# Token tiles one column later, an earlier load, and expert lists kept in SBUF: three edits in an encoder block

## The reference, cut to what matters

```python
mixed = sigmoid(g_a) * (o_g @ w_o_gqa) + sigmoid(g_b) * (o_m @ w_o_mla)
h = h + mixed @ w_out
t = rmsnorm(h, ffn_norm)
aff = softmax(t @ w_router, axis=-1)            # 16 experts
g, idx = top_k(aff.T, 130)                      # each expert picks 130 tokens
xs = t[idx]
y = (silu(xs @ w_gate) * (xs @ w_up)) @ w_down  # hidden width 512
h = h.at[idx].add(y * g[..., None])
```

## Time and profile before

| what | value |
|---|---|
| median of the runs (lowest, highest) | 2949.36 us (2943.27, 2949.93) |
| the profiled execution's own time | 2949.2 us |
| its span, first to last instruction | 2947.4 us |
| TensorE busy | 2790.1 us, 95% |
| VectorE, ScalarE, GpSimd busy | 61%, 49%, 25% |
| mean granted TensorE clock | 0.972 of full speed |
| mixing, last pass ends; residual; selection; experts begin | about 1931, to 2178, to 2225, 2242 us |

### The profile page before, as it was taken

One profiled execution on the slowest core, in us unless ns is written; L12 is line 12 of the kernel. 1 busy time (PEld: TensorE's weight loads), 2 busy tenths in 40 slices (PEclk: granted clock), 3 DMA queues, 4 the chain that ended last, 5 costly groups with the idle time before them and its releaser, 6 DMA issues. The chain is left out here.

```text
span 2947.4 us, 54402 instructions
## 1 busy us (share of the span) xinstructions
PE 2790.1 (95%) x19748; PEld 2613.7 (89%) x19748; DVE 1811.8 (61%) x2888; ACT 1448.8 (49%) x2623; POOL 740.9 (25%) x1279
## 2 busy tenths in 40 slices
PE   8999899999999999999999999999946999999994
PEld 7888698999989999999999999988836999999994
DVE  6777766888887777775343334423354565555555
ACT  4333336888887777776222223311122445444543
POOL 0000013444442554546000000000031333323331
PEclk9999898999999999999999999999977999999997
DMA  6556493112204334553865754556645898888977
GB/s 210 154 157 191 143 385 111 49 47 73 52 23 101 90 100 127 138 148 104 239 183 162 212 161 136 143 180 195 198 126 138 203 211 200 201 198 215 204 160 266
DMA packets 534413, 466.64 MB, mean 158 GB/s; under 512 B 61907, under 2 KB 467107, under 8 KB 534257
## 3 DMA queue, kind: packets, MB, share of 16 engines
q1 hardware_dynamic: 510768, 403.68, 47.9%
q0 software_dynamic: 21120, 60.81, 9.1%
q10 hardware_dynamic: 2368, 0.16, 0.0%
HBM read 320.29 MB, written 144.21 MB: 158 GB/s over the span
## 5 line engine op out<-in xcount | busy, mean ns | idle before, releaser
L2835 PE MATMUL e_gu<-e_x_hi,w_hi 128*128 128x260 f32 x1024 | 294.2, 287 | 0.9 <-DVE e_x_lo L3040 0.9
L2835 PE MATMUL e_gu<-e_x_lo,w_hi 128*128 128x260 f32 x1024 | 290.3, 284 | 0.0
L2835 PE MATMUL e_gu<-e_x_hi,w_lo 128*128 128x260 f32 x1024 | 290.0, 283 | 0.0
L3035 DVE TENSOR_TENSOR w_lo<-w_raw,w_hi 128x2048 fp32r<-128x2048 f32 x90 | 206.3, 2292 | 100.5 <-ACT w_hi L2936 99.7
L1956 ACT ACTIVATE n_exps<-n_st_ps 128x348 f32<-128x348 f32 (+3 forms) x432 | 199.0, 461 | 120.5 <-PE n_st_ps L1901 116.0
L2039 DVE TENSOR_TENSOR n_p_lo<-n_exps,n_p_hi 128x696 fp32r<-128x696 f32 (+1 forms) x192 | 176.3, 918 | 106.4 <-ACT n_p_hi L1970 106.1
L123 POOL MEMSET s_ident<- 128x128 f32 x1 | 0.2, 209 | 779.2 <-POOLq L3247 779.2
L2835 PEld LDWEIGHTS e_gu<-e_x_hi,w_hi 128*128 128x128 f32 x1024 | 194.1, 190 | 1.1 <-DVE e_x_lo L3040 1.1
L2835 PEld LDWEIGHTS e_gu<-e_x_lo,w_hi 128*128 128x128 f32 x1024 | 194.3, 190 | 0.0
L2835 PEld LDWEIGHTS e_gu<-e_x_hi,w_lo 128*128 128x128 f32 x1024 | 193.9, 189 | 0.0
L2236 PE MATMUL c_acc<-c_tokens,c_w_back 128*128 128x260 f32 x1536 | 191.2, 284 | 2.9 <-DVE c_prod L2311 2.8
(11 more groups left out here) (344 smaller groups left out, 7751.0 us busy)
## 6 DMA issues: line engine op xcount, KB each, us to landing
c_raw<-in_w_in SPq DMA_DIRECT2D x64, 512.0 KB, 5.2
w_raw<-in_w_gate SPq DMA_DIRECT2D x64, 512.0 KB, 6.5
w_raw<-in_w_up SPq DMA_DIRECT2D x64, 512.0 KB, 8.0
w_raw<-in_w_down SPq DMA_DIRECT2D x64, 512.0 KB, 4.5
c_tokens<-hn_t SPq DMA_DIRECT2D x16, 1040.0 KB, 9.6
c_tokens<-o_t SPq DMA_DIRECT2D x32, 520.0 KB, 6.6
r_mt<-mix_t SPq DMA_DIRECT2D x32, 512.0 KB, 5.2
mix_t<-c_out_hi SPq DMA_DIRECT2D x32, 260.0 KB, 2.1
```

The lines of the kernel that those rows point to most:

```text
L2835: ins = pe.matmul(gu[:, j % 2, a, 0:W], w[:, j, at:at + P], t[:, k, :], start=(k == 0 and q == 0), stop=(k == DK - 1 and q == 2))
L3035: dve.tensor_tensor(w_lo[:, j, :], raw[:, j % RAW, :], w_hi[:, j, :].bitcast(F32), ALU.subtract)\
```

## The change

It has three parts. In the experts, column m of the down product is followed by tile m + 1 for m from 1 to 6, on TensorE, ScalarE and VectorE; the places of the late slabs stay as they were.

In mixing and residual, SP's wait for the last stores is taken out of mixing. Residual's SP waits for mixing's last product instead, loads mixed tile and `x` of tile 1, then `x` of tile 0, the gain row and the router, and only then waits for the stores.

For the lists, a tensor `aff_home` of 64 half lists of 528 columns lies at a fixed place of SBUF through residual and selection. The first halves hold the meta tokens and four tiles, the second halves four tiles and 16 columns that GpSimd sets to -1. List tiles of the steps before step 11 still go to `aff_t`; at step 11 SP waits for those stores and issues four DMAs that bring them home; the later tiles are stored straight into `aff_home`. The selection has no load of the lists, and VectorE waits for `row_map` only behind the 17 rounds.

```diff
 mix, SP:
-            sp.wait_ge(stored, 32 * DK * PASSES)
...
 residual, SP:
+            def load_home(s):
+                for g in range(GROUPS):
+                    tiles = (s - g + 1) // 2
+                    sp.wait_ge(aff_stored[g], 16 * tiles)
+                    late = (tiles - XCH // 2) * P
+                    back = (GROUPS + g) * E
+                    sp.dma_start(aff_home[g * E:(g + 1) * E, META:], scr["aff_t"][g * E:(g + 1) * E, META:FIRST_HALF])\
+                        .then_inc(gain_loaded, 16)
+                    sp.dma_start(aff_home[back:back + E, 0:late],
+                                 scr["aff_t"][g * E:(g + 1) * E, FIRST_HALF:FIRST_HALF + late]).then_inc(gain_loaded, 16)
+
+            sp.wait_ge(*mixed_done["products"])
+            load(1, 1)
             load(0, 0)
-            load(1, 1)
             sp.dma_start(gain[:, :], spread(io["ffn_norm"][0, :], 0, P)).then_inc(gain_loaded, 16)
             sp.dma_start(router[:, :, :], io["w_router"][0].rearrange("(k p) e -> p k e", p=P)).then_inc(router_loaded, 16)
+            sp.wait_ge(*mixed_done["stored"])
...
+                    if isinstance(s, int) and s == DIRECT:
+                        load_home(s)
...
+                    elif isinstance(s, int) and s >= DIRECT:
+                        first, at = (GROUPS + g) * E, (tile_index(s, g) - XCH // 2) * P
+                        sp.dma_start(aff_home[first:first + E, at:at + P], aff_rows[:, g, :]).then_inc(aff_stored[g], 16)
...
+            pool.wait_ge(router_loaded, 16)
+            pool.memset(aff_home[GROUPS * E:, XCH // 2 * P:], -1.0).then_inc(router_loaded, 1)
...
 choose, SP and VectorE:
-            for part in range(2):
-                sp.dma_start(aff[part * LISTS:(part + 1) * LISTS, :], scr["aff_t"][:, part * HALF:(part + 1) * HALF])\
-                    .then_inc(loaded, 16)
...
-            dve.wait_ge(loaded, 48)
...
             link(dve.tensor_copy(column[:, :], index[:, :]))
+            dve.wait_ge(loaded, 16)
...
 experts, TensorE:
-                    if not is_last(e) and m + 2 < DK:
-                        tokens_of(e + 1, m + 2)
+                    if not is_last(e) and 1 <= m < DK - 1:
+                        tokens_of(e + 1, m + 1)
...
 experts, ScalarE and VectorE, in both alike:
-                    if m + 2 < DK:
-                        tokens(e + 1, m + 2)
+                    if 1 <= m < DK - 1:
+                        tokens(e + 1, m + 1)
                     if m in LATE_SLABS:
                         slab(e + 1, LATE_SLABS[m])
```

More of the change, by code:

```diff
@@ L2343, in _, with residual @@
                     body(DK - 1, 1, True)
-    return dict(products=(prod_done, NB * DK * PASSES), first_products=(prod_done, NB * DK * PASSES - 1),
+    return dict(stored=(stored, 32 * DK * PASSES), products=(prod_done, NB * DK * PASSES), first_products=(prod_done, NB * DK * PASSES - 1),
                 out_weights=(out_split_lo, DK))
-def residual(nc, io, scr, block, ident, w_out, loads, mixed_done, passed):
+AFF_AT = 226304
+def residual(nc, io, scr, aff_home, block, ident, w_out, loads, mixed_done, passed):
     N = STEPS
@@ L2399, in residual @@
         LOADS = 16 * 2
+        DIRECT = N - 6
         @block.sync
@@ L2440, in body @@
                     wait_alone(sp, at_copied, s + 1, sp_passed)
+                    if isinstance(s, int) and s == DIRECT:
+                        load_home(s)
                     if isinstance(s, int) and s == N - 1:
                         for gg in range(GROUPS):
-                            sp.dma_start(scr["aff_t"][gg * E:(gg + 1) * E, 0:META],
+                            sp.dma_start(aff_home[gg * E:(gg + 1) * E, 0:META],
                                          aff_rows[:, g, gg * META:(gg + 1) * META]).then_inc(aff_stored[g], 16)
+                    elif isinstance(s, int) and s >= DIRECT:
+                        first, at = (GROUPS + g) * E, (tile_index(s, g) - XCH // 2) * P
+                        sp.dma_start(aff_home[first:first + E, at:at + P], aff_rows[:, g, :]).then_inc(aff_stored[g], 16)
                     else:
@@ L2454, in _ @@
             sp.wait_ge(aff_stored[1], 16 * (N // 2))
+            sp.wait_ge(gain_loaded, 16 + 32 * GROUPS)
+            sp.wait_ge(router_loaded, 17)
+        @block.gpsimd
+        def _(pool):
+            pool.wait_ge(router_loaded, 16)
+            pool.memset(aff_home[GROUPS * E:, XCH // 2 * P:], -1.0).then_inc(router_loaded, 1)
         @block.tensor
@@ L2573, in _, with choose @@
             steps(dve, body, 1, 3)
-def choose(nc, io, scr, rows_t, gates_t, out_rows, w_raw, w_hi, w_lo):
+FIRST_HALF = META + TOK // 256 * P
+def choose(nc, io, scr, aff, rows_t, gates_t, out_rows, w_raw, w_hi, w_lo):
     LISTS = GROUPS * E
     ROUNDS = (CAP + 7) // 8
-    HALF = TOK // 2
     with ExitStack() as ctx:
@@ L2588, in sem @@
             return nc.alloc_semaphore("s_" + name)
-        aff = sb("aff", [2 * LISTS, HALF])
         top, index = sb("top", [2 * LISTS, ROUNDS * 8]), sb("index", [2 * LISTS, ROUNDS * 8], U32)
@@ L3239, in row_map @@
     front = np.stack([x_offset, meta_offset - x_offset], axis=1)
-    back = np.stack([x_offset + TOK // 2, 0 * x_offset], axis=1)
+    back = np.stack([x_offset + FIRST_HALF, 0 * x_offset], axis=1)
     return np.concatenate([front, back]).astype(np.float32)
@@ L3245, in build @@
     scr = scratch_tensors(nc)
+    aff_home = nc.alloc_sbuf_tensor_at("aff_home", [2 * GROUPS * E, FIRST_HALF], F32, offset=AFF_AT)
     with nc.cleanup_on_exit(), ExitStack() as ctx:
@@ L3262, in build @@
         mixed_done = mix(nc, io, scr, block, mix_loads, attended, w_out, residual_loads, passed)
-        residual(nc, io, scr, block, ident, w_out, residual_loads, mixed_done, passed)
+        residual(nc, io, scr, aff_home, block, ident, w_out, residual_loads, mixed_done, passed)
     with ExitStack() as ctx:
@@ L3271, in build @@
         w_lo = weights.at((RAW + SLABS) * SLAB, "w_lo", [P, SLABS, SLAB], F32R)
-        choose(nc, io, scr, rows_t, gates_t, out_rows, w_raw, w_hi, w_lo)
+        choose(nc, io, scr, aff_home, rows_t, gates_t, out_rows, w_raw, w_hi, w_lo)
         experts(nc, io, scr, outs, rows_t, gates_t, out_rows, weights, w_raw, w_hi, w_lo)
```

## The result

The changed kernel takes **2983.51 us** (median of four runs, 2980.45 to 2985.53) against 2949.14 for the kernel before in the same comparison (2943.27 to 2949.93). The ratio is 1.0119, 95% interval 1.0102 to 1.0135: it is slower by some 35 us. The profiled execution took 2984.78 us for a span of 2983.0, against 2949.2 and 2947.4 before.

The account below looks back on a forecast made before the run. TensorE, busy 95% of the span, was taken as the bound. Experts + 21.3, residual - 6.15 and selection - 2.2 made + 12.9 us on 2949.4, forecasting 2962 us, range 2953 to 2983.

Parts of the forecast that it names:

- the clock: At 14 expert boundaries, a fall behind the new wait was priced at nothing; the other end was + 20.4 us.
- The clock falls too: Rival: clock falls at most of the 14 expert boundaries, + 13 to + 20 us more, 2975 to 2983; chance 0.30.
- The wait at the gate product: At 14 expert boundaries, TensorE waits 1.97 us for tile 7's x_lo, queued behind slab 4; each boundary grows by 1.55.
- + 18 to + 25: Range in us for the 14 expert boundaries together, with every release 0.05 to 0.1 quicker or slower; central value + 21.7.
- The boundary into the last expert: The 15th boundary: slab 4 starts earlier, so the copy of column 7 comes sooner, - 0.4 us.
- Residual: Second mixed tile loaded earlier, removing TensorE's wait and the clock's fall: - 6.15 us, at least - 2.5.
- the rival of 2.5: Rival in residual: the early load does not help, giving back only 2.5 us, total 2966; chance 0.07.
- its sign: In residual, the forecast itself expected the second split to start without a wait and at full clock.
- Selection: First max no longer waits for lists, - 2.79 us; wider passes cost at most + 0.54; together - 2.2.
- Sum: Whole kernel: experts + 21.3, residual - 6.15, selection - 2.2, together + 12.9 us, giving 2962.
- Tile 7 is hidden anyway: Rival at expert boundaries: gate product does not wait, each boundary gains 0.42 us, total about 2935; chance 0.06.

Follow-up runs that it names:

- Experiment 2: Changed kernel with 14 useless products behind column 7, filling TensorE's wait before the gate product: 2963.87 us, ratio 1.0064.
- the experts' order alone: Kernel before the change with only the later order of the token tiles in the experts: 2988.41 us, ratio 1.0146.
- experiment 3: Changed kernel with 5 useless products behind column 7, filling part of TensorE's wait before the gate product: 2964.78 us, ratio 1.006.
- experiment 1: Changed kernel with slab 4 moved from m = 5 to m = 6, behind tile 7: 2935.24 us, ratio 0.9964; timed again 2936.78 us.
- experiment 6: Experiment 1's kernel with slabs 4 and 5 of the last expert split in that expert, behind the results: 2934.64 us, ratio 0.9962.
- experiment 7: Experiment 6's kernel with the fourth hidden tile ahead of row squares, first roots and first normalized row: 2935.95 us, ratio 0.996.
- the experts' order undone: Changed kernel with the old order of token tiles in the experts, keeping early load and lists in SBUF: 2938.51 us, ratio 0.9973.
- selection alone: Kernel before the change with only the lists in SBUF: 2944.09 us, ratio 0.9996.
- residual alone: Kernel before the change with only the early loads of mixing and residual: 2942.11 us, ratio 0.9985.

## Why the prediction was wrong, point by point

The direction and the place were right, the time was 21.5 us too low (2962 against 2983.5), just beyond the upper end of 2983.

**The step that failed is the clock.** The prediction said of it: "A wait of 1.97 is nearer to that one, so I price the fall at nothing". Measured: 12 falls at 14 boundaries, 1.50 each against the 1.46 worked out from the earlier trace rows, and a thirteenth at the last boundary for 0.34, together 18.3 us. Experiment 2 shows this by itself: with the wait filled and the gate product no sooner, that time goes. The rival "The clock falls too" (2975 to 2983) was what happened; its price was right, its chance too low. The argument by the nearest row failed because one row of each kind (2.35 with a fall, 2.04 without) was taken to give a length from which the clock falls, and a wait below the row without a fall was then called safe. The 2.04 wait was a single event, and it gives no such length: ahead of the same transposes a wait of 2.07 in the changed kernel, and of 2.06 in the experts' order alone, was followed by half clock. Why 2.04 was not stays open. The Trainium skill, "TensorE: Matmul & The Clock Gate", section "HAM oscillation", tells of a loop whose DMA waits, some 3 to 5 us long, bring the clock down anew in every tile. The runs show the same for a wait that returns with every expert and is shorter, 1.87 to 1.89, in 12 of 14, and not for the 1.27 of experiment 3.

**The wait at the gate product** was right: predicted 1.97, measured 1.87, at all 14. From T2, T5 was forecast 5.48 later and came 5.45 later, T6 7.22 and 7.24, and x_lo of tile 7 stood 4.87 behind T6 as forecast. The boundary grew by 1.79, not 1.55: 0.12 at T2, which comes later behind the rest of column 1, and 0.10 in the steps behind it, most of it the release from x_lo to the gate product, 0.66 for 0.58. Over 14 boundaries that is 25.1, the upper end of "+ 18 to + 25".

**The boundary into the last expert** was forecast at - 0.4. Where no fall lies in its period (experiments 2 and 3) that period is 48.14 against 48.39 before: - 0.25.

**Residual** was right by the trace: 6.30 for the forecast 6.15 between the first and the third product of a mixed tile. The run of that part alone gives 4.4 with 6.15 inside its interval; the rival of 2.5 is inside it too, but its sign (a wait for `r_mt`) is absent from the trace.

**Selection**: forecast - 2.2 (- 2.8 to - 1.5), by the trace - 1.8; the stores into SBUF, taken at 0, cost 0.5 at the barrier (4.29 against 3.79).

**Sum.** With the measured terms: 14 x 1.79 + 18.3 - 0.25 - 6.3 - 1.8 = + 35.0, for a span 35.6 longer. Two differences outside these terms nearly cancel: residual is reached 2.3 later, and what follows the last gate product is 1.3 shorter. "Tile 7 is hidden anyway", the rival on the other side, forecast about 2935 for slab 4 out of the way; experiment 1, which puts it out of the way, measured 2935.24. That the two agree so well is luck: the rival was 14.7 less than before, and experiment 1 is 10.5 less than its own runs of before. A full boundary gained 0.35 instead of 0.42, and the last one lost 1.8 where - 0.4 was taken.

## What to carry to other kernels

When a step is moved along in a program with in-order queues, look at what the move puts ahead of it on the engine that releases the bound: here one entry of a dictionary, unchanged, came to stand between a tile and the product that waits for it, and one edit of it was worth 46 to 48 us. A new wait that returns with every pass has two prices, the wait itself and the clock behind it; take in both unless waits of that length at such a place are seen many times without a fall. And an operation taken out of one queue position has to be followed to its next one: experiments 6 and 7 won 5 us at a boundary, and lost 3 of them in the one and as good as all in the other behind the next queue.

## What the runs showed of the hardware

The length of a wait does not by itself say whether the clock falls. Waits of 1.87 to 1.89 were followed by half clock at 12 of 14 boundaries in both kernels that have them, and the two spared, six boundaries apart, had waits as long. A wait of 1.27 at the same place was not followed by it, at any of 14 boundaries. At the boundary into the last expert 2.07 and 2.06 were followed by it in the same two kernels, and 2.04 ahead of the same transposes kept full clock before the change, with the experts' order undone, in selection alone and in residual alone:

```profile
2856.55 1.06 PE L2851 MATMUL e_tp<-e_ident,e_y_t 128*65 128x128 f32 x8 [2.04 <-issue]
...
2859.69 1.09 PE L2851 MATMUL e_tp<-e_ident,e_y_t 128*65 128x128 f32 x8 [1.21 <-ACT e_y L2966]
```

```profile
2856.00:2858.00 2.00, 1.45 (x14) 1.48 (x15) 1.97 (x3) 0.44 (x1) 0.15 (x1) 1.00 0.00 0
2858.00:2860.00 2.00, 0.79 (x8) 0.54 (x7) 1.96 (x4) 1.04 (x2) 0.00 (x0) 1.00 0.00 0
```

What sets them apart was not tried, but it is not chance alone: in the changed kernel each fall comes about 0.25 nearer to the start of the gate product than the one an expert before, until it comes at the start itself; the next boundary is spared, and behind that the falls begin again about a microsecond behind the start. The clock of the first 1.2 us at four boundaries in a row shows it:

```profile
2412.51:2413.71 1.20, 1.20 (x6) 1.20 (x7) 1.20 (x2) 0.06 (x1) 0.90 (x2) 0.61 0.46 135
2457.12:2458.32 1.20, 1.20 (x5) 1.20 (x6) 1.20 (x2) 0.05 (x1) 0.90 (x2) 0.51 0.44 133
2501.71:2502.91 1.20, 1.20 (x10) 1.20 (x11) 1.20 (x2) 0.06 (x1) 0.89 (x2) 1.00 0.45 135
2544.81:2546.01 1.20, 1.20 (x9) 1.20 (x10) 1.20 (x2) 0.06 (x1) 0.90 (x2) 0.95 0.34 104
```

Both kernels have this order. So when a wait comes seems to count beside how long it is; this is read from the order alone, and no run tested it.

Filling a wait with useless products kept the clock up at no cost in time: with 5 or with 14 of them the boundary took the same 43.1.
